# A hybrid attention decoder on one core: the sum of the first squares, a pair of key copies and two remainders put elsewhere in their engines' programs

## The chip, the cores and the metric

The kernel runs on one core of one Trainium2 chip. The metric is the device time of one execution in microseconds, the median of three runs. Engines are named as in the profile: PE is TensorE, DVE is VectorE, ACT is ScalarE, POOL is GpSimd and SP is SyncE.

## What is computed

x is 1 x 1024 x 1024 in float32. Two layers, each of a mixer and a gated feed-forward part, then a last norm:

```
for layer in range(2):
    hn = rms_norm(h, norm_mix_g[layer])
    h = h + hybrid_mixer(hn, ...)      # hn @ w_in, 2 units of dilated attention, 4 of differential, 2 of short convolution, @ w_out
    hn = rms_norm(h, norm_ffn_g[layer])
    g, u = split(hn @ w_up)            # 2816 columns each
    h = h + (silu(causal_dwconv(g)) * u) @ w_down
return rms_norm(h, final_g)
```

Before the mixer's attention, the first quarter of every head's dimensions is turned by angles that come from the positions (sine and cosine tables).

## The kernel before

Features lie on the partitions, the 1024 tokens along the rows. Every float32 operand of a large product is split in two: a head (rounded, `_hi`) and a rest (what is left, `_lo`), and each product is three matmuls: head by head, rest by head, head by rest. A weight block has its head made by a rounding on ACT (line 1825) or POOL, and its rest by a subtraction on POOL (line 762, `rest_of_block`; it writes `w_lo`). When a rest is done, POOL raises `block_ready` (line 765), for which PE waits before it uses the block.

Five engines run programs of their own, written out by hand in Python, and meet by semaphores alone. What stands first in an engine's program is issued first: an instruction that waits holds back everything behind it on its engine.

**The start.** ACT rounds the eight tiles of x of the first half of the tokens to `x_hi` and squares them, then does the same for the second half. DVE makes the rests `x_lo` of the first half (`absorb(0, ...)`), then four tiny products for lambda, then the angles (`angles`, 14 small instructions on 128x128, lines 2580 to 2605), then the rests of the second half (`absorb(1, ...)`), and then `partial(0, 0, 1)`: seven additions (line 2082) that sum the squares of the first half into one tile. PE (`start_normed`, line 1278) sums that tile over the partitions (line 1229), after which DVE takes the roots (`roots(0)`), PE spreads them (line 1275) and ACT keeps them. `partial(0, 1, 1)` and `roots(1)` do the same for the second half. The first projections are under way meanwhile; POOL splits each weight tile (`split`, lines 727 and 729) once PE has freed the place.

**The first unit of attention.** ACT, in the first step of unit 0: it keeps the turned probabilities (line 1693), v, the exponentials of step 1, then copies the second half of q (`keep_q`, lines 1732 and 1733) and of k (`cross_k`, lines 1737 and 1738) to where the score products read them, then the second turned group, and last the head's output (`keep_head`, line 1753).

**The feed-forward part.** The 22 hidden tiles are taken as 11 pairs; products are done in Strassen's manner, with seven instead of eight block products. For each of the first ten pairs of a layer the down projection has four mixed operands, T1 to T4, which POOL forms (line 833, `form`) and ACT rounds (line 1870); POOL then makes their rests (line 837, `rest_formed`). T2 is kept with its sign turned, for which ACT overwrites it after T4 is formed from it (`negate_t2`, line 1876, which raises `t2_negated`). In the program of POOL, for an even tile, these stand in this order:

```
                        form_t2_t3(layer, pair)
                        later_weights(1)
                        form_t4(layer, pair)
                        rest_t3(layer, pair)
                        rest_t2(layer, pair)
                        later_weights(1)
```

Then come `rest_t4` and four more weight blocks. `rest_t3` waits for T3's rounding, `rest_t2` for `t2_negated`. On PE, `part_b` (line 1146) takes the blocks S2, A12, S3, S4, A22 in turn, with four rows of three matmuls each (lines 1126 to 1128); ahead of S2 it waits for the block and for `t_rested` to have counted T1's, T2's and T3's rests together, ahead of A12 for that block:

```
                pe.wait_ge(block_ready, s2 + 1)
                pe.wait_ge(t_rested, 4 * done + 3)
```

DVE, in the same stretch, has two taps of the convolution (line 2491, three operands in SBUF) and the additions to h (line 1989, one operand in PSUM).

Of the kernel before, what the change touches and what calls it, by code (L numbers as in the profile page):

```python
# [18 lines left out]
KT = D_MODEL // P  # L19
# [248 lines left out]
def build(nc, x_t, positions, stream, vectors, first_g, rope, identity, causal, dilation, out_t):  # L268
# [9 lines left out]
    with ctx:  # L278
# [431 lines left out]
        def _(pool):  # L710
# [150 lines left out]
            def form_t4(layer, pair):  # L861
                pool.wait_ge(t_formed, 4 * (layer * (PAIRS - 1) + pair) + 3)
                form("T4", mixed_raw["T2"], k_next[:, 0:HALF])

            def rest_t3(layer, pair):
                pool.wait_ge(t_rounded, 4 * (layer * (PAIRS - 1) + pair) + 3)
                rest_formed("T3")

            def rest_t2(layer, pair):
                pool.wait_ge(t2_negated, layer * (PAIRS - 1) + pair + 1)  # L870
                rest_formed("T2")
# [56 lines left out]
            for layer in range(DEPTH):  # L928
                for n in range(len(PROJECTIONS) + 1):
                    split()  # L930
                    if n == 1:
                        zeros(layer)
                    for name, j in jobs_of_step(n - 3):
                        sum_part(layer, name, j)

                pool.wait_ge(tables_saved, 32)
                pool.wait_ge(next_ready, 2 * (layer + 1) * ATTENDING)
                split_mix(layer, SPLIT_BY_POOL[0])
                pool.wait_ge(half_done, layer * LAYER_HALVES + PROJECTED)
                for m in SPLIT_BY_POOL[1:]:  # L940
                    split_mix(layer, m)
                pool.wait_ge(prob_ready, plain_steps(layer, FINAL, 2))
                for _ in range(len(OUT_TILES) - 3):
                    split()
                sum_ffn(layer)
                split()
                for what, n in feed_forward():
                    pair = (n - 1) // 2
                    if what == "down":
                        later_weights(4)  # L950
                    elif what == "part_a":
                        if n == 0:
                            form_t1(layer, 0)
                            later_weights(1)
                            rest_t1(layer, 0)
                            later_weights(1)
                        else:
                            later_weights(2)
                    elif what == "part_b":
                        rest_t4(layer, n)  # L960
                        later_weights(4)
                    elif n == 0:

                        first_weights(layer)
                    elif n > 1 and n % 2 == 0:
                        later_weights(PRODUCTS - 1)
                        form_t2_t3(layer, pair)
                        later_weights(1)
                        form_t4(layer, pair)
                        rest_t3(layer, pair)  # L970
                        rest_t2(layer, pair)
                        later_weights(1)
                    elif n > 1:
                        later_weights(PRODUCTS - 1)
                        if n < F_TILES - 1:
                            form_t1(layer, (n - 1) // 2)
                        later_weights(1)
                        if n < F_TILES - 1:
                            rest_t1(layer, (n - 1) // 2)
# [575 lines left out]
        def _(act):  # L1555
# [147 lines left out]
            def keep_mix(layer, u):  # L1703
                act.wait_ge(heads_turned, seen(heads_turned))
                by = 1.0 if u < A_UNITS else gain_of(layer, V_SUBLN_SCALED, 0)
                if u >= PENULTIMATE:
                    for t in range(2):
                        act.activation(x_hi[:, u, halves_of_t[t]], bank(IDLE[t]), ACT.Copy, scale=by)\
                           .then_inc(final_hi if u == FINAL else penultimate_hi, 1)
                else:  # L1710
                    if layer:
                        act.wait_ge(h_saved[u], 16 * layer)
                    for t in range(2):
                        act.activation(h[:, u, halves_of_t[t]], bank(IDLE[t]), ACT.Copy, scale=by)\
                           .then_inc(mix_kept, 1)
# [19 lines left out]
            def cross_k(attended, part=slice(0, SEQ)):  # L1735
                act.wait_ge(next_ready, 2 * attended + 2)
                act.activation(k_twice[high, 0, part], k_next[low, part], ACT.Copy).then_inc(hi_kept, 1)
                act.activation(k_twice[low, 1, part], k_next[high, part], ACT.Copy).then_inc(hi_kept, 1)
# [8 lines left out]
            def keep_head(g, i, u):  # L1747
                heads, dilated = heads_of(u), u < A_UNITS
                act.wait_ge(head_done, g + 1)
                act.wait_ge(share_ready, g + 1)  # L1750
                if dilated:
                    for j in range(2):
                        act.activation(heads[:, i, HEAD_DIM * j:HEAD_DIM * (j + 1)],
                                       ps[:, HEAD, HEAD_DIM * j:HEAD_DIM * (j + 1)], ACT.Copy,
                                       scale=share[:, g % 2, j:j + 1]).then_inc(head_out, 1)
                else:
                    act.activation(heads[:, i, :], ps[:, HEAD, 0:P], ACT.Copy, scale=share[:, g % 2, 0:1])\
                       .then_inc(head_out, 1)
                    act.activation(ps[:, HEAD, P:2 * P], ps[:, HEAD, 0:P], ACT.Square,
                                   scale=share[:, g % 2, 0:1], accum_out=head_sums[:, u // FINAL, i:i + 1]).then_inc(head_out, 1)  # L1760
# [14 lines left out]
            def attention(layer):  # L1775
                attended = layer * ATTENDING
                if layer:
                    load_table(ACT.Exp)
                keep_first(layer)
                exps(step_of(layer, 0, 0), 0)  # L1780
                for u in range(ATTENDING):
                    dilated = u < A_UNITS
                    for i in range(QB):
                        g, many = step_of(layer, u, i), len(groups(i, dilated))
                        keep_turned(g, i, dilated, 0)
                        if i == 0:
                            keep_v()
                        if i < QB - 1:
                            exps(g + 1, i + 1)
                        if u == 0 and i == 0:  # L1790
                            keep_q(attended, halves_of_t[1])
                            cross_k(attended, halves_of_t[1])
                        if u < FINAL and i == QB - 2:
                            keep_q(attended + u + 1)
                        if u < FINAL and i == QB - 1:
                            cross_k(attended + u + 1)
                        if u and i == turning_step(u):
                            keep_mix(layer, u - 1)
                        if u == FINAL and i == 0:
                            split_second_channel(layer)  # L1800
                            scale_heads(layer)
                        for n in range(1, many):
                            keep_turned(g, i, dilated, n)
                            if u < FINAL and i == QB - 1 and n == max(1, many - 2):
                                exps(g + 1, 0)
                        keep_head(g, i, u)
                keep_mix(layer, FINAL)

            def conv_center(out, tap):
# [150 lines left out]
        def _(dve):  # L1960
# [16 lines left out]
            def absorb(t, order, g_of):  # L1977
                for m in order:
                    dve.wait_ge(x_hi_ready, seen(x_hi_ready))
                    dve.scalar_tensor_tensor(x_lo[:, m, halves_of_t[t]], h[:, m, halves_of_t[t]], g_of(m),  # L1980
                                             x_hi[:, m, halves_of_t[t]].bitcast(f32),
                                             ALU.mult, ALU.subtract).then_inc(x_lo_ready, 1)
# [653 lines left out]
            for layer in range(DEPTH):  # L2636
                for n in range(2):
# [2 lines left out]
                                      vec[:, layer, c + 1:c + 2], ALU.mult).then_inc(dve_seq, 1)  # L2640
                    dve.wait_ge(dve_seq, seen(dve_seq))
            dve.sem_inc(lam_ready, 1)
            angles()
            absorb(1, range(KT), g_of)
            dve.wait_ge(eye_in, 16)
            partial(0, 0, 1)
            roots(0)
            partial(0, 1, 1)
            dve.wait_ge(rstd_ready, seen(rstd_ready))
# [99 lines left out]
```

## Time and profile before

| what | us |
|---|---|
| median of 3 runs (2380.68 to 2384.05) | 2381.22 |
| the profiled execution's own time | 2382.89 |
| its span | 2381.1 |
| PE busy with matmuls | 2338.4 |
| DVE busy | 1633.0 |
| POOL busy | 1291.0 |
| ACT busy | 990.3 |

The profiled execution is one run, 1.67 us above the median. Its span lies 1.8 us below its own time; that remainder is outside the program's instructions. Busy times of engines overlap. Start times are counted from the start of the span, and "idle before" is the time the engine stood still ahead of an instruction, with what released it behind an arrow.

### The profile page before, as it was taken

How to read it: one execution, taken by the hardware profiler on the slowest of the kernel's cores; microseconds unless marked ns; L12 is line 12 of the kernel's file. 1: busy time of each engine (PE TensorE's matmuls, PEld its weight loads, DVE VectorE, ACT ScalarE, POOL GpSimd, SP SyncE). 2: the span in 40 equal slices, each digit the busy share in tenths (PEclk: the TensorE clock that was granted, in tenths of full speed). 3: DMA queues.
4: the chain of work that ended last, by engine and by line, in shares of the span. 5: the costliest groups of instructions: out<-in, count | busy, mean ns of one | idle time of the engine just before them, and what ended most of it. 6: DMA issues, size and time to landing. Idle time of an engine off the chain costs nothing.

```text
span 2381.1 us, 32322 instructions
## 1 busy us (share of the span) xinstructions
PE 2338.4 (98%) x11340; PEld 1952.4 (82%) x11340; DVE 1633.0 (69%) x2648; ACT 990.3 (42%) x1906; POOL 1291.0 (54%) x893
## 2 busy tenths in 40 slices
PE   7999999999999999999999999999999999999998
PEld 6888888877788888888878888888777888888886
DVE  8744677738767777667795457785496677777775
ACT  4344444525434344344524344444254333433343
POOL 3222323448776667777542223242687777677764
PEclk9999999999999999999999999999999999999999
DMA  8957796421333333333399659852223333333332
GB/s 280 246 140 174 187 223 136 118 62 41 101 95 101 96 96 98 97 94 98 131 282 219 168 145 223 191 105 83 62 67 93 98 96 99 99 94 101 99 100 77
DMA packets 162768, 304.47 MB, mean 128 GB/s; under 512 B 11440, under 2 KB 31024, under 8 KB 162608
## 3 DMA queue, kind: packets, MB, share of 16 engines
q1 hardware_dynamic: 129408, 238.20, 32.3%
q0 software_dynamic: 31616, 62.92, 14.7%
q8 instruction: 92, 1.51, 0.3%
q10 hardware_dynamic: 1584, 1.28, 0.2%
q14 instruction: 68, 0.56, 0.1%
HBM read 292.66 MB, written 135.27 MB: 180 GB/s over the span
## 4 chain that ended last, share of the span: by engine, by line
PE 84%; DVE 8%; POOL 4%; issue 2%; ACT 1%; DMA 1%; DVEq 0%; SPq 0%; POOLq 0%; ACTq 0%
PE ps L1048 11%; PE ps L1049 11%; PE ps L1050 11%; PE ps L1019 7%; PE ps L1021 7%; PE ps L1020 7%; PE ps L1126 5%; PE ps L1128 5%; PE ps L1127 5%; PE ps L1367 5%; PE ps L1354 3%; PE ps L1341 2%; PE ps L1342 2%; POOL w_lo L762 1%; DVE q_next L2082 1%
## 5 line engine op out<-in xcount | busy, mean ns | idle before, releaser
L762 POOL TENSOR_TENSOR w_lo<-more_stage,w_hi 128x512 fp32r<-128x512 f32 x304 | 431.8, 1420 | 193.8 <-ACT w_hi L1825 178.4
L727 POOL CAST w_hi<-stage 128x1024 fp32r<-128x1024 f32 x68 | 71.0, 1044 | 650.1 <-PE ps L1021 575.5
L1019 PE MATMUL ps<-x_hi,w_hi 128*128 128x512 f32 x928 | 373.0, 402 | 2.1 <-POOLq L732 1.0
L1021 PE MATMUL ps<-x_hi,w_lo 128*128 128x512 f32 x928 | 362.9, 391 | 0.0
L1020 PE MATMUL ps<-x_lo,w_hi 128*128 128x512 f32 x928 | 361.6, 390 | 0.0
L1825 ACT ACTIVATE w_hi<-more_stage 128x512 fp32r<-128x512 f32 x294 | 181.8, 626 | 290.2 <-PE ps L1050 205.7
L1989 DVE TENSOR_TENSOR h<-ps,h 128x512 f32<-128x512 f32 x400 | 254.1, 683 | 39.7 <-PE ps L1128 30.1
L1048 PE MATMUL ps<-T_hi,w_hi 128*128 128x512 f32 x688 | 267.9, 389 | 1.5 <-DVE q_next L2457 1.5
L1050 PE MATMUL ps<-T_hi,w_lo 128*128 128x512 f32 x688 | 267.7, 389 | 0.0
L1049 PE MATMUL ps<-T_lo,w_hi 128*128 128x512 f32 x688 | 267.7, 389 | 0.0
L762 POOL TENSOR_TENSOR w_lo<-stage,w_hi 128x512 fp32r<-128x512 f32 x146 | 197.7, 1354 | 128.8 <-ACT w_hi L1825 121.5
L1048 PE MATMUL ps<-B_hi,w_hi 128*128 128x512 f32 x552 | 216.3, 392 | 0.0
L1049 PE MATMUL ps<-B_lo,w_hi 128*128 128x512 f32 x552 | 214.8, 389 | 0.0
L1050 PE MATMUL ps<-B_hi,w_lo 128*128 128x512 f32 x552 | 214.8, 389 | 0.0
L1019 PEld LDWEIGHTS ps<-x_hi,w_hi 128*128 128x128 f32 x928 | 174.5, 188 | 38.8 <-issue 4.4
L1021 PEld LDWEIGHTS ps<-x_hi,w_lo 128*128 128x128 f32 x928 | 174.2, 188 | 38.1
L1020 PEld LDWEIGHTS ps<-x_lo,w_hi 128*128 128x128 f32 x928 | 174.7, 188 | 34.6 <-issue 1.2
L1126 PE MATMUL ps<-mix,w_hi 128*128 128x512 f32 x480 | 187.2, 390 | 3.1 <-POOLq L765 3.1
L1693 ACT ACTIVATE padded<-ps 128x512 f32<-128x512 f32 (+2 forms) x192 | 94.4, 492 | 229.9 <-PE ps L1354 229.8
L1127 PE MATMUL ps<-mix,w_hi 128*128 128x512 f32 x480 | 186.8, 389 | 0.0
L1128 PE MATMUL ps<-mix,w_lo 128*128 128x512 f32 x480 | 186.8, 389 | 0.0
L729 POOL TENSOR_TENSOR w_lo<-stage,w_hi 128x1024 fp32r<-128x1024 f32 x68 | 170.1, 2501 | 5.5
(281 smaller groups left out, 4950.5 us busy)
## 6 DMA issues: line engine op xcount, KB each, us to landing
summed<-stream SPq DMA_DIRECT2D x40, 1024.0 KB, 9.3
more_stage<-stream SPq DMA_DIRECT2D x128, 256.0 KB, 2.7
stage<-stream SPq DMA_DIRECT2D x52, 512.0 KB, 3.9
more_stage<-summed SPq DMA_DIRECT2D x100, 256.0 KB, 2.6
summed_downs<-stream SPq DMA_DIRECT2D x16, 1280.0 KB, 10.6
summed<-stream POOLq DMA_DIRECT2D x20, 1024.0 KB, 15.1
summed<-summed POOLq DMA_DIRECT2D x20, 1024.0 KB, 13.2
more_stage<-summed_downs SPq DMA_DIRECT2D x60, 256.0 KB, 2.6
```

The lines of the kernel that those rows point to most:

```text
L762: pool.tensor_tensor(block_of(w_lo, n), raw, block_of(w_hi, n).bitcast(f32), ALU.subtract)\
L1019: pe.matmul(out, w_hi[:, s, w], hi, start=start, stop=False)
L1020: pe.matmul(out, w_hi[:, s, w], lo, start=False, stop=False)
L1021: return pe.matmul(out, w_lo[:, s, w], hi, start=False, stop=stop)
L1048: pe.matmul(out, block_of(w_hi, n)[:, columns], hi, start=start, stop=False)
L1049: pe.matmul(out, block_of(w_hi, n)[:, columns], lo, start=False, stop=False)
L1050: return pe.matmul(out, block_of(w_lo, n)[:, columns], hi, start=False, stop=stop)
L1126: pe.matmul(bank(b), block_of(w_hi, n)[:, columns], hi, start=start, stop=False, skip_group_check=True)
L1127: pe.matmul(bank(b), block_of(w_hi, n)[:, columns], lo, start=False, stop=False, skip_group_check=True)
L1128: pe.matmul(bank(b), block_of(w_lo, n)[:, columns], hi, start=False, stop=True, skip_group_check=True)\
L1825: act.activation(block_of(w_hi, at), raw_block(layer, n), ACT.Copy).then_inc(block_hi, 1)
L1989: dve.tensor_tensor(row, bank(b), row, ALU.add).then_inc(add_done, 1)
```

## The change

Three edits, each a move within one engine's program; nothing is added or taken away.

- POOL, in each of the 20 pairs with mixed operands: T2's rest now stands ahead of T3's.
- ACT, in the first step of unit 0 of each layer: the copies of k's second half now stand behind the first head's output instead of right behind q's.
- DVE, at the start: the seven additions of the first half's squares now stand ahead of the second half's rests, and the angles behind those.

```diff
@@ -967,8 +967,8 @@
                         form_t2_t3(layer, pair)
                         later_weights(1)
                         form_t4(layer, pair)
+                        rest_t2(layer, pair)
                         rest_t3(layer, pair)
-                        rest_t2(layer, pair)
                         later_weights(1)
@@ -1789,7 +1789,6 @@
                         if u == 0 and i == 0:
                             keep_q(attended, halves_of_t[1])
-                            cross_k(attended, halves_of_t[1])
@@ -1804,6 +1803,8 @@
                         keep_head(g, i, u)
+                        if u == 0 and i == 0:
+                            cross_k(attended, halves_of_t[1])
                 keep_mix(layer, FINAL)
@@ -2640,10 +2641,10 @@
             dve.sem_inc(lam_ready, 1)
+            partial(0, 0, 1)
+            absorb(1, range(KT), g_of)
             angles()
-            absorb(1, range(KT), g_of)
             dve.wait_ge(eye_in, 16)
-            partial(0, 0, 1)
             roots(0)
```

POOL in a pair of the feed-forward part, before, from the forming of T2 and T3 (line 833) on; `mix` and `mix_raw` hold T2 and T3, `t_raw` T4:

```order
L833 TENSOR_TENSOR mix_raw<-k_next,mix_raw 128x512 [waits pool_seq,t_rested,value_ready]
L833 TENSOR_TENSOR mix_raw<-k_next,mix_raw 128x512 [waits b12_kept]
L762 TENSOR_TENSOR w_lo<-stage,w_hi 128x512 [waits block_hi]
L833 TENSOR_TENSOR t_raw<-mix_raw,k_next 128x512 [waits pool_seq,t_formed]
L837 TENSOR_TENSOR mix<-mix_raw,mix 128x512 [waits t_rounded]
L837 TENSOR_TENSOR mix<-mix_raw,mix 128x512 [waits t2_negated]
```

And the same place with the change:

```order
L833 TENSOR_TENSOR t_raw<-mix_raw,k_next 128x512 [waits pool_seq,t_formed]
L837 TENSOR_TENSOR mix<-mix_raw,mix 128x512 [waits t2_negated]
L837 TENSOR_TENSOR mix<-mix_raw,mix 128x512 [waits t_rounded]
L762 TENSOR_TENSOR w_lo<-more_stage,w_hi 128x512 [waits block_hi]
L837 TENSOR_TENSOR t_lo<-t_raw,t_hi 128x512 [waits pool_seq,t_rounded]
L762 TENSOR_TENSOR w_lo<-stage,w_hi 128x512 [waits block_hi]
```

The instruction that waits for `t2_negated` now stands first, and the one that waits for T3's rounding behind it; the block rests (S2's, T4's rest, A12's) follow as before.

DVE at the start with the change, from the products for lambda on (line numbers are one higher than before; `heads` holds the angles):

```order
L2640 TENSOR_TENSOR heads<-vec 128x1 [waits dve_seq] x3
L2083 TENSOR_TENSOR q_next<-k_next,q_next 128x512 [waits dve_seq,squares_ready0]
L2083 TENSOR_TENSOR q_next<-v_next,q_next 128x512 [waits squares_ready0,dve_seq]
L2083 TENSOR_TENSOR q_next<-v_cur,q_next 128x512 [waits squares_ready0,dve_seq]
L2083 TENSOR_TENSOR q_next<-padded,q_next 128x512 [waits squares_ready0,dve_seq]
L2083 TENSOR_TENSOR q_next<-prob,q_next 128x512 [waits squares_ready0,dve_seq] x3
L1981 SCALAR_TENSOR_TENSOR x_lo<-h,gain,x_hi 128x512 [waits x_hi_ready] x8
L2583 CAST heads<-heads 128x128 [waits pos_in]
```

Before, the angles (the cast and the 13 behind it) stood first, then the eight rests, then the seven additions, with the roots behind them; the roots now follow the angles.

## Rows read from the trace of the kernel before

**Rows 1.** The page, its first part: busy time, share of the span, instructions of each engine.
```profile
PE 2338.4 (98%) x11340; PEld 1952.4 (82%) x11340; DVE 1633.0 (69%) x2648; ACT 990.3 (42%) x1906; POOL 1291.0 (54%) x893
```

**Rows 2.** Waits of PE, whole span: total us, times, longest.
```profile
PE ps L1126 <- POOLq L765: 3.1, 4, 1.2
```

**Rows 3.** PE, groups of instructions, 640 to 1180 us: busy, mean ns, idle before.
```profile
L1126 PE MATMUL ps<-mix,w_hi 128*128 128x512 f32 x216 | 84.0, 389 | 0.0
```

**Rows 4.** POOL, timeline around the third pair of layer 0: start, us, instruction, idle before.
```profile
705.02 1.30 POOL L762 TENSOR_TENSOR w_lo<-more_stage,w_hi 128x512 fp32r<-128x512 f32 x1 [1.33 <-ACT w_hi L1825]
...
722.89 3.52 POOL L833 TENSOR_TENSOR mix_raw<-k_next,mix_raw 128x512 f32<-128x512 f32 x2 [0.24 <-POOL w_lo L762]
...
729.08 2.56 POOL L837 TENSOR_TENSOR mix<-mix_raw,mix 128x512 fp32r<-128x512 f32 x2
731.60 1.30 POOL L762 TENSOR_TENSOR w_lo<-more_stage,w_hi 128x512 fp32r<-128x512 f32 x1
733.08 1.29 POOL L837 TENSOR_TENSOR t_lo<-t_raw,t_hi 128x512 fp32r<-128x512 f32 x1 [0.18 <-POOL w_lo L762]
734.32 1.29 POOL L762 TENSOR_TENSOR w_lo<-stage,w_hi 128x512 fp32r<-128x512 f32 x1
735.79 2.06 POOL L762 TENSOR_TENSOR w_lo<-stage,w_hi 128x512 fp32r<-128x512 f32 x1 [0.18 <-POOL w_lo L762]
```

**Rows 5.** ACT, timeline of the same stretch.
```profile
704.31 0.63 ACT L1825 ACTIVATE w_hi<-more_stage 128x512 fp32r<-128x512 f32 x1 [2.09 <-PE ps L1050]
...
729.16 0.63 ACT L1876 ACTIVATE mix_raw<-mix_raw 128x512 f32<-128x512 f32 x1 [1.57 <-POOL t_raw L833]
```

**Rows 6.** PE, timeline: the first rows of S2 and of A12, same pair.
```profile
733.97 0.39 PE L1126 MATMUL ps<-mix,w_hi 128*128 128x512 f32 x1
...
736.69 0.39 PE L1126 MATMUL ps<-mix,w_hi 128*128 128x512 f32 x1
```

**Rows 7.** DVE, timeline of the same pair.
```profile
723.54 1.72 DVE L2042 TENSOR_TENSOR mix<-k_next,mix 128x1024 fp32r<-128x1024 f32 x1
...
734.85 1.85 DVE L2491 SCALAR_TENSOR_TENSOR k_next<-padded,vec,k_next 128x1024 f32<-128x1024 f32 x1
```

**Rows 8.** Line 833 on POOL, all pairs: duration ns least/median/most.
```profile
L833 POOL TENSOR_TENSOR mix_raw<-k_next,mix_raw x40: 1287/1783/2316, 608.7 to 2293.8; 128x512 f32<-128x512 f32 x40
```

**Rows 9.** POOL, DVE and PE, timelines of the first pair of layer 0.
```profile
617.43 1.29 POOL L762 TENSOR_TENSOR w_lo<-more_stage,w_hi 128x512 fp32r<-128x512 f32 x1
...
618.37 1.43 DVE L2491 SCALAR_TENSOR_TENSOR k_next<-padded,vec,k_next 128x1024 f32<-128x1024 f32 x1
...
618.82 0.50 PE L1126 MATMUL ps<-mix,w_hi 128*128 128x512 f32 x1 [1.17 <-POOLq L765]
...
622.30 0.50 PE L1126 MATMUL ps<-mix,w_hi 128*128 128x512 f32 x1 [0.43 <-POOLq L765]
```

**Rows 10.** DVE, timeline of the start.
```profile
17.36 0.23 DVE L2582 CAST heads<-heads 128x128 f32<-128x128 int32 x1
...
21.27 5.39 DVE L1980 SCALAR_TENSOR_TENSOR x_lo<-h,gain,x_hi 128x512 fp32r<-128x512 f32 x8 [0.16 <-DVE heads L2603]
...
29.46 2.76 DVE L2082 TENSOR_TENSOR q_next<-padded,q_next 128x512 f32<-128x512 f32 x1
...
45.01 2.15 DVE L2082 TENSOR_TENSOR q_next<-prob,q_next 128x512 f32<-128x512 f32 x3
```

**Rows 11.** POOL and PE, timelines of the start.
```profile
28.96 2.70 POOL L729 TENSOR_TENSOR w_lo<-stage,w_hi 128x1024 fp32r<-128x1024 f32 x1
...
34.45 1.87 PE L1229 MATMUL ps<-ones,q_next 128*128 128x1 f32 x8 [3.46 <-DVE q_next L2082]
```

**Rows 12.** Busy by stretch: us, PE, PEld, DVE, ACT, POOL, PEclk, DMA share, GB/s.
```profile
34.40:38.00 3.60, 3.54 (x12) 3.20 (x13) 1.36 (x10) 0.00 (x0) 0.00 (x0) 0.50 1.03 380
```

**Rows 13.** PE, timeline of step 1 of unit 0, layer 0.
```profile
78.44 0.43 PE L1367 MATMUL ps<-v_cur,padded 128*128 128x64 f32 x2 [1.68 <-ACT padded L1693]
...
79.29 0.47 PE L1019 MATMUL ps<-x_hi,w_hi 128*128 128x512 f32 x1 [0.19 <-DVE q_next L1966]
```

## The prediction

> **What bounds the kernel now.** I read the page first, then PE's waits, then the timelines of the three places that the change touches. PE is busy for 98% of the span [rows 1], so whatever makes PE stand still is added to the time, and only an idle stretch of PE can be won. Of PE's waits two matter here: 3.46 us at the start for the squares that DVE sums [rows 11], and, in the list by releaser, 3.1 us for weight blocks from POOL, in four places [rows 2]. Those four are two each in the first pair of either layer [rows 9]. In the other pairs PE waits for nobody: the groups of 640 to 1180 us show no idle time ahead of the down rows [rows 3]. The question for POOL's edit is thus how much room the other 18 pairs have.
>
> **POOL: T2's rest ahead of T3's, 20 times.** PE asks for three rests by one count, so T2's rest being early wins nothing: both must be done. What changes is a wait. Before, POOL went from forming T4 (ends about 729.1) straight to T3's rest, and the two rests took 729.08 to 731.64 [rows 4]. ACT turned T2's sign from 729.16 to 729.79 [rows 5], under cover of T3's rest. Now POOL stands at T2's rest until that is done. A POOL instruction that waits for ACT starts 0.08 after ACT's end (704.94 to 705.02, [rows 4, 5]), so the rests start at 729.87 instead of 729.08: 0.79 late, with nothing to hide it on POOL. Queued behind are S2's block rest, T4's rest, A12's and S3's block rests [rows 4].
> - S2: its rest would end at 731.60 + 1.30 + 0.79 = 733.69. PE starts 0.10 after such an end (618.72 to 618.82, [rows 9]), so at 733.79; it came at 733.97 [rows 6]. Covered, by 0.18.
> - T4's rest moves to 733.87 to 735.16.
> - DVE's tap is issued at 734.85 [rows 7], by PE's progress and so as before. Today it falls into A12's block rest, is held until that ends at 735.61 and itself ends at 736.70, 1.09 later. Held behind it, S3's block rest ends at 737.85, 1.15 after the tap [rows 4]. PE has room there.
> - Now the tap falls into T4's rest instead, ahead of A12's. It gets its turn at 735.16 and ends at 736.25; A12's block rest, issued back to back, waits for it and ends at 737.40. PE can start A12 at 737.50 and needs it at 736.69 [rows 6]: a new wait of 0.81.
>
> That DVE goes in between two back-to-back POOL instructions is the step that decides. It is read from forming T2 and T3: together 3.52 instead of twice 1.29 [rows 4], with DVE's 723.54 instruction ending at 725.26, 1.08 after T2's [rows 7]. It is no single case: the median of 40 such POOL instructions is 1783 ns [rows 8], between a short first one and a long second one, in all 18 of the later pairs.
>
> The Trainium skill ("SBUF — State Buffer", section "SBUF: two separate sides") says of the port pair which DVE and GpSimd share that whoever starts first has it for the whole instruction, and speaks of deep queues that the hardware does not drain. Read strictly, POOL's next instruction, already queued, might go first; the sum of this part would then be 1.6 us, not 16.2. The rows above speak for the turn passing to DVE, and I go by them.
>
> So 18 later pairs x 0.81 = 14.6 us. In the first pairs the same shift meets no room: S2's rest now ends at 619.51, and the tap of 618.37 is held until then instead of 618.72 [rows 9], so T4's rest and A12's block rest also come 0.79 late. PE's start of A12 moves from 622.30 to 623.09, its earlier wait for S2 growing by the same 0.79 and not adding to it. Twice 0.8 is 1.6 us. Sum: **+16.2 us**. Bounds: 0 if A12 still comes in time everywhere, and 20 x 1.09 = 21.8 if the whole tap fell on PE.
>
> **DVE: the first squares' sum moved ahead.** Today PE stands 3.46 us for it [rows 11]. Now DVE adds from about 17.4: seven additions at 0.72 ([rows 10]: three in 2.15) end at 22.4. Eight rests at 0.67 [rows 10] end at 27.8, against 26.66 today; PE needs them and comes 1.2 us later, then does 3.6 us of heads and the sums by 32.9 without a wait. POOL's split of the third tile, released by PE, runs 28.7 to 32.9 and holds up DVE: an addition beside it took 2.76 [rows 10, 11]. It now falls on the angles (3.8 us, today 17.36 to 21.11, [rows 10]), which end between 31.6 and 35.5. The roots take 3.1 us, from 33.0 or 35.5. The second sum then meets POOL's next split (35.0 to 39.2) and ends at about 43.8 in both cases, since what is not held in the one is held in the other. Today it ends at 47.16 [rows 10]: 3.3 us won.
>
> Part of that is given back. PE has nothing to do from about 39.3 to 44, which is longer than the 3.46 us after which its granted clock stood at 0.50 [rows 12], 1.2 instead of 2.4 GHz, where sums took 1.87 [rows 11] instead of about 1. A like stretch would now follow the second sum; today's falls where DVE is the slower chain anyway. It takes up to 2.7 us of PE's time, of which PE's chain has about 0.8 to spare before it is the later one. I take 1.3 for it: **-2.0 us**. Bounds: -3.3 (no slow stretch) and +0.5 (the slow stretch hits PE's heads after 27 too, and the second sum comes as late as today). The tables of sine and cosine are issued some 7 us later but still land by 43, 5 us ahead of their use.
>
> **ACT: k's copies behind the first head, twice.** PE's wait of 1.68 us for the turned group [rows 13] goes, since those copies stood ahead of it. But PE's next projection starts at 79.29, when DVE has emptied its bank [rows 13], and DVE waits for none of the moved instructions. PE then waits 2 us for DVE instead. k's copies come 0.7 us later and are asked for two steps on. I take **0**; bounds -1.7 and +0.7 each time.
>
> **Sum:** 16.2 - 2.0 + 0 = +14.2 us. The profiled execution's 2382.89 becomes 2397.1; against the median of 2381.22, which is 1.67 lower, I forecast **2395.4 us**.
>
> **The rivals.**
> - A: POOL keeps its turn. Its next instruction goes ahead of DVE's tap, A12's rest ends at 736.4 and PE finds it ready at 736.69. Then the 18 later pairs cost nothing, and 1.6 - 2.0 = -0.4 leaves 2380.8, not slower. It decides at one point: whether a DVE instruction that waits 0.31 us already gets in. For it: the wait is shorter than the 0.64 in the forming of T2 and T3. Against it: the turn passed each time there. 0.10.
> - B: as forecast, but the start wins nothing, because PE's clock falls in the sparse stretch after 25 or the angles hold up roots and tables. +16.2 to +16.7: 2397.9. 0.15.
> - C: the tap itself comes later than 735.16 in some pairs, or DVE's being done 0.45 earlier is handed on to POOL, so that about half of the waits appear: 8.1 - 2.0 = +6.1, 2387.3. 0.08.
> - D: PE's waits are made good later in the pair, because ACT or DVE is the true limit. Against it, no idle time at all ahead of PE's instructions [rows 3]. Then only the start counts: -2.0 to -3.3, 2378.6. 0.03.
>
> **How the numbers follow.** The forecast has 0.64, B 0.15, C 0.08, A 0.10, D 0.03. The forecast's terms reach from 14.6 + 1.6 - 3.3 = +12.9 to 16.2 + 0.5 = +16.7; widened for PE's wait by 0.15 us a pair (3 us) this is 2391 to 2401. Reaching toward C, I give 2389 to 2400. This measurement can tell about 0.2%, 4.8 us, from no change. Slower by more: forecast, B and most of C, 0.86. Within: A, D and the rest, 0.12. Faster: 0.02.
>
> **What would show it.** PE's waits should name POOL's line 765 ahead of line 1126 some 20 to 24 times, 0.8 us each, at A12; POOL should stand 0.7 us ahead of line 837, released by ACT's line 1876, 20 times; A12's block rest should last over 2 us, and S3's 1.3. At the start PE's wait for the first sum should be gone and that for the second be over 4 us, and the second sum should end near 44. If POOL's A12 rest lasts 1.3 us, the step on the turn is wrong; if PE waits at S2, the room of 0.18 was misread.

## The result, and the profile after

| what | before | after |
|---|---|---|
| median, us (6 runs each, taken together) | 2380.95 (2378.03 to 2384.51) | 2397.32 (2394.93 to 2399.63) |
| the profiled execution's own time, us | 2382.89 | 2398.16 |
| its span, us | 2381.1 | 2396.4 |

The changed kernel is slower: the ratio is 1.0063, with a 95% interval of 1.0053 to 1.0073. That is 15.0 us on 2381.22; the two medians of the table lie 16.4 us apart. Below, a difference from the kernel before is likewise its ratio's share of the median of before, and a difference between two changed kernels is one of medians. The forecast was 2395.4 us with a range of 2389 to 2400 and a chance of 0.86 for slower.

The page of the changed kernel, first part, and below it one line of its list of PE's waits (total us, times, longest). Where line numbers stand behind the change on ACT, they are one higher than before.

```profile
PE 2347.3 (98%) x11340; PEld 1954.3 (82%) x11340; DVE 1645.4 (69%) x2648; ACT 989.9 (41%) x1906; POOL 1305.3 (54%) x893
```

```profile
PE ps L1126 <- POOLq L765: 15.0, 21, 1.9
```

POOL and DVE are busy 14.3 and 12.4 us longer than in [rows 1] with the same number of instructions: they hold each other up for longer. PE's wait for weight blocks was 3.1 us in four places [rows 2], and is now 15.0 in 21. It is there in every pair. Here is PE from 640 to 1180 us, the stretch whose groups had no idle time [rows 3]:

```profile
L1126 PE MATMUL ps<-mix,w_hi 128*128 128x512 f32 x216 | 85.3, 395 | 5.5 <-POOLq L765 5.5
```

POOL's timeline in one pair, the fourth of layer 0; it answers to [rows 4].

```profile
783.16 1.29 POOL L833 TENSOR_TENSOR t_raw<-mix_raw,k_next 128x512 f32<-128x512 f32 x1 [0.18 <-POOL w_lo L762]
785.19 2.56 POOL L837 TENSOR_TENSOR mix<-mix_raw,mix 128x512 fp32r<-128x512 f32 x2 [0.74 <-ACT mix_raw L1877]
787.71 1.29 POOL L762 TENSOR_TENSOR w_lo<-more_stage,w_hi 128x512 fp32r<-128x512 f32 x1
789.17 1.29 POOL L837 TENSOR_TENSOR t_lo<-t_raw,t_hi 128x512 fp32r<-128x512 f32 x1 [0.18 <-POOL w_lo L762]
790.41 2.27 POOL L762 TENSOR_TENSOR w_lo<-more_stage,w_hi 128x512 fp32r<-128x512 f32 x1
792.86 1.30 POOL L762 TENSOR_TENSOR w_lo<-more_stage,w_hi 128x512 fp32r<-128x512 f32 x1 [0.18 <-POOL w_lo L762]
```

DVE and PE in the same pair, from their timelines; the first answers to [rows 7], the second to [rows 6].

```profile
790.16 1.38 DVE L2492 SCALAR_TENSOR_TENSOR k_next<-padded,vec,k_next 128x1024 f32<-128x1024 f32 x1
```

```profile
789.28 0.39 PE L1126 MATMUL ps<-mix,w_hi 128*128 128x512 f32 x1
...
792.79 0.50 PE L1126 MATMUL ps<-mix,w_hi 128*128 128x512 f32 x1 [0.62 <-POOLq L765]
793.12 0.39 PE L1127 MATMUL ps<-mix,w_hi 128*128 128x512 f32 x1
```

This is how the chain reads. POOL stands 0.74 at T2's rest. T4's rest lies at 789.17 to 790.46. The tap of DVE is issued in it, at 790.16, takes its turn when T4's rest ends and is done at 791.54. A12's block rest, begun on paper at 790.41, takes 2.27 instead of 1.29 us: it was held for DVE. It ends at 792.68 and PE starts A12 at 792.79. S2 came without a wait, and S3's block rest takes 1.30, where before it was the held one with 2.06 [rows 4].

At the start, the rows of DVE (timeline) that answer to [rows 10], and PE's and the busy time by stretch that answer to [rows 11, 12]:

```profile
22.20 5.38 DVE L1981 SCALAR_TENSOR_TENSOR x_lo<-h,gain,x_hi 128x512 fp32r<-128x512 f32 x8
...
28.60 0.94 DVE L2591 TENSOR_SCALAR heads<-heads 128x128 f32<-128x128 f32 x1
29.58 3.16 DVE L2594 SCALAR_TENSOR_TENSOR heads<-heads 128x128 f32<-128x128 f32 x3
...
41.05 2.14 DVE L2083 TENSOR_TENSOR q_next<-prob,q_next 128x512 f32<-128x512 f32 x3
```

```profile
31.72 0.95 PE L1229 MATMUL ps<-ones,q_next 128*128 128x1 f32 x8
...
43.25 1.86 PE L1229 MATMUL ps<-ones,q_next 128*128 128x1 f32 x8 [3.64 <-DVE q_next L2083]
```

```profile
44.00:50.00 6.00, 6.00 (x20) 5.01 (x20) 4.76 (x18) 0.00 (x0) 0.00 (x0) 0.60 1.10 269
```

The first sum costs PE no wait any more. The second ends at 43.19 instead of 47.16, PE has stood 3.64 us for it, and the granted clock over 44 to 50 us is 0.60 in the mean, which means that most of them ran at 1.2 GHz.

To see where the time goes between these places I took a mark that all kernels have, the end of ACT's sign change of T2 in each pair, and subtracted its time before from its time after. The differences were -5.26 us in the first pair of layer 0, -3.67 in the second, +4.01 in the tenth; +4.71, +5.49 and +12.92 in the same pairs of layer 1; the span ends at +15.3. From one pair to the next it grows by 0.96 on average in layer 0 and by 0.93 in layer 1 (single steps of 0.90 to 1.17). So the profiled execution won about 5 us at the start, lost 19.4 in the pairs (1.6 and 0.8 in the two first ones, 18 x 0.94 in the others) and about 1 elsewhere. The 5 us hold for this pair of executions: the section on DVE's edit shows that the profiled execution of the kernel before was the slowest of five up to the first pair.

### The profile page after: what moved, and what is told of

The parts are those of the page before. It is cut to its first block, busy times and chain, and to the rows that moved or that the text cites. A ratio compares the mean times of both kernels' runs of the same rounds, so it can differ in the third digit from the quotient of the medians.

```text
span 2396.4 us, 32322 instructions
## 1 busy us (share of the span) xinstructions
PE 2347.3 (98%) x11340; PEld 1954.3 (82%) x11340; DVE 1645.4 (69%) x2648; ACT 989.9 (41%) x1906; POOL 1305.3 (54%) x893
## 3 DMA queue, kind: packets, MB, share of 16 engines
q0 software_dynamic: 31616, 62.92, 14.6%
## 4 chain that ended last, share of the span: by engine, by line
PE 72%; POOL 15%; DVE 7%; issue 2%; ACT 2%; DMA 1%; POOLq 0%; DVEq 0%; SPq 0%; ACTq 0%
PE ps L1048 8%; PE ps L1050 8%; PE ps L1049 8%; PE ps L1019 7%; PE ps L1021 7%; PE ps L1020 7%; POOL w_lo L762 6%; PE ps L1126 5%; PE ps L1367 5%; PE ps L1127 5%; PE ps L1128 5%; POOL mix_raw L833 3%; PE ps L1354 3%; POOL mix L837 2%; PE ps L1341 2%
## 5 line engine op out<-in xcount | busy, mean ns | idle before, releaser
L762 POOL TENSOR_TENSOR w_lo<-more_stage,w_hi 128x512 fp32r<-128x512 f32 x304 | 446.2, 1468 | 194.7 <-ACT w_hi L1826 181.1
```

What stands on the lines that cost most here:

```text
L762: pool.tensor_tensor(block_of(w_lo, n), raw, block_of(w_hi, n).bitcast(f32), ALU.subtract)\
```

## The experiments

Two theories were to be told apart for POOL's edit: that the turn on what POOL and DVE share passes to DVE between T4's rest and A12's block rest (mine), and that POOL is simply later all the way, in proportion to its wait. For the start it was to be seen how much of the won time is given back. Each kernel below was run 11 times, POOL's edit alone 4 times and the filling of 720 elements 5 times. The kernel before was run 27 times beside each of the two groups: their medians are 2382.20 for the first four kernels below and 2382.23 for the last four.

### POOL's edit alone

```diff
                         form_t4(layer, pair)
+                        rest_t2(layer, pair)
                         rest_t3(layer, pair)
-                        rest_t2(layer, pair)
```

> The kernel before with T2's rest ahead of T3's alone. Theory (the tap takes the turn ahead of A12's block rest): PE waits at A12 in each of the 18 later pairs; the two traces give 0.94 us a pair there (period 57.12 before, 58.05 with the change) and about 2.4 us in the two first pairs, so +19 us over before, more than the whole change cost. Rival (my own sum on record): +16. Rival that the start or ACT's edit carries the loss: 0 to +3.

Measured: 2401.92 us (2399.25 to 2403.11), ratio 1.0082 (1.0068 to 1.0096), which is +19.5 us on 2382.20. PE's waits in its profile:

```profile
PE ps L1126 <- POOLq L765: 14.5, 21, 1.9
```

The mark grows by 0.98 us a pair in layer 0 and by 0.95 in layer 1, much as in the changed kernel. POOL's edit alone makes the loss, and more than the whole change lost.

### DVE's edit alone

```diff
+            partial(0, 0, 1)
+            absorb(1, range(KT), g_of)
             angles()
-            absorb(1, range(KT), g_of)
             dve.wait_ge(eye_in, 16)
-            partial(0, 0, 1)
             roots(0)
```

> The kernel before with DVE's edit at the start alone. The traces of before and of the change put DVE's evacuation in step 1 of unit 0 at 78.45 and 73.53, and the first pair at 615.6 and 610.4: theory -5 us, kept to the end. Rival (my sum on record): -2, because the granted clock falls after PE's longer wait for the second sum. Rival that the won time is lost again before the end: 0.

Measured: 2377.43 us (2376.49 to 2380.34), ratio 0.9981 (0.9973 to 0.9990), -4.5 us (interval -6.4 to -2.4). First the two traces, that of before and this one. Before, PE at the second spreading of the roots and at step 1 of unit 0 (beside [rows 13]):

```profile
53.69 1.02 PE L1275 MATMUL ps<-q_next,ones 128*128 128x512 f32 x2
...
61.73 0.47 PE L1019 MATMUL ps<-x_hi,w_hi 128*128 128x512 f32 x1 [0.17 <-DVE q_next L1966]
65.37 0.30 PE L1341 MATMUL ps<-k_twice,q_split 128*128 128x128 f32 x1 [0.68 <-DVEq L2148]
```

With DVE's edit alone, PE at the same two places:

```profile
52.95 1.02 PE L1275 MATMUL ps<-q_next,ones 128*128 128x512 f32 x2
...
75.01 0.47 PE L1019 MATMUL ps<-x_hi,w_hi 128*128 128x512 f32 x1
```

At the spreading only 0.74 us are left of the 3.91 by which the second sum came earlier (43.30 against 47.21, both in PE's timelines): PE is busy all the while, but from 44 to 50 us at a granted clock of 0.50, so the low clock has taken the rest, and more than the 1.3 of the estimate. But at the projection of step 1 PE is 4.28 us ahead (75.01 against 79.29 [rows 13]). In between PE stood before for 0.17 + 0.68 + 1.68 + 0.19 = 2.72 us, three times for DVE and once for ACT, which itself waited for DVE's turned k. With DVE's edit none of the four waits is there.

It would be wrong to put the gain down to these four waits, since other executions with the old order at the start do not have them either. Here is step 1's projection in the kernel with a filling of 310 elements (further below), which leaves the start as it was (its line 1024 is line 1019 of before):

```profile
78.23 0.47 PE L1024 MATMUL ps<-x_hi,w_hi 128*128 128x512 f32 x1
```

And the busy time by stretch, 33 to 55 us, of the kernel before, of that kernel, and of DVE's edit alone (the seventh figure is the granted clock):

```profile
33.00:55.00 22.00, 18.33 (x72) 14.43 (x73) 18.80 (x45) 0.85 (x2) 7.14 (x4) 0.84 0.68 204
33.00:55.00 22.00, 17.88 (x63) 14.20 (x64) 18.85 (x45) 0.60 (x1) 6.77 (x4) 0.77 0.76 221
33.00:55.00 22.00, 18.35 (x68) 14.11 (x67) 19.69 (x54) 3.67 (x7) 6.33 (x4) 0.84 1.06 278
```

Four profiled executions have the old order at the start besides that of before: POOL's edit alone, ACT's edit alone and the two fillings. In all four the mean granted clock of this stretch is 0.77. The clock falls twice there, for 10.2 us together, where the trace of before has one fall of 6.8 us. PE then stands nowhere between 50 and 90 us, and step 1's projection starts at 77.27 to 78.27. The four executions with the new order (DVE's edit alone, it with ACT's, the changed kernel, and A12's rest put first) each have one fall of 6.8 us, and that projection starts at 74.37 to 75.01. Against the four others the new order is thus 3.1 us ahead there, on average, without any of the 2.72. The low stretch after the longer wait is no new cost against them: they had one about the second sum too, and one more before it. At the mark in the first pair of layer 0 the five old orders stand at 613.26 to 615.63, with before the last of them, and the four new ones at 610.38 to 611.27: 3.6 us between the means. Why the clock falls twice in some executions and once in another of the same order is not shown.

### ACT's edit alone

```diff
                             keep_q(attended, halves_of_t[1])
-                            cross_k(attended, halves_of_t[1])
...
                         keep_head(g, i, u)
+                        if u == 0 and i == 0:
+                            cross_k(attended, halves_of_t[1])
```

> The kernel before with k's copies behind the first head alone. Theory: PE no longer waits 1.7 us for the turned group in step 1 but then waits for DVE's evacuation instead, in both layers: 0 us, within 0.5. Rival: the copies held PE up for good, -1.7 to -3.4 us.

Measured: 2381.98 us (2377.24 to 2384.65), ratio 0.9999 (0.9990 to 1.0007). PE's waits in its profile:

```profile
PE ps L1019 <- DVE q_next L1967: 2.3, 2, 2.1
```

In the kernel before, the waits ahead of line 1367 for ACT were 4.0 us, here they are 0.6; those ahead of line 1019 for this DVE line were 0.8, here 2.3. In layer 1 a wait is renamed, as the sum had it: 1.68 for ACT and 0.20 for DVE became 2.15 for DVE. In layer 0 this trace shows neither wait, and nor do three others that have the old start, so they can't show the renaming there. The time says 0, with an interval of -2.4 to +1.7 us.

### A12's block rest ahead of T4's rest

To the changed kernel; POOL does A12's rest before T4's.

```diff
                     elif what == "part_b":
+                        later_weights(1)
                         rest_t4(layer, n)
-                        later_weights(4)
+                        later_weights(3)
```

> The changed kernel, and A12's block rest ahead of T4's rest on POOL in every part b. POOL is as late as in the changed kernel (0.79 us at T2's rest), but the tap now falls into A12's block rest, which so ends in time. Theory of the turn: PE waits at A12 in no later pair, T4's rest is the one that stands behind the tap, where PE has room: -17 us against the changed kernel, about 2379 to 2381. Rival (POOL's lateness as such is paid, wherever it stands): as the changed kernel, 2396.

Measured: 2380.88 us (2378.66 to 2384.95), ratio 0.9997 (0.9988 to 1.0006). POOL's timeline in the fourth pair, and PE's waits:

```profile
783.99 2.56 POOL L837 TENSOR_TENSOR mix<-mix_raw,mix 128x512 fp32r<-128x512 f32 x2 [0.74 <-ACT mix_raw L1878]
786.51 1.29 POOL L762 TENSOR_TENSOR w_lo<-more_stage,w_hi 128x512 fp32r<-128x512 f32 x1
787.98 1.29 POOL L762 TENSOR_TENSOR w_lo<-more_stage,w_hi 128x512 fp32r<-128x512 f32 x1 [0.18 <-POOL w_lo L762]
789.44 2.06 POOL L837 TENSOR_TENSOR t_lo<-t_raw,t_hi 128x512 fp32r<-128x512 f32 x1 [0.18 <-POOL w_lo L762]
```

```profile
PE ps L1127 <- POOLq L765: 3.7, 2, 1.9
```

POOL is as late as in the changed kernel (0.74), and PE waits in no pair but the first of each layer. Lateness in itself costs nothing in the 18; what costs is that the block PE needs next stands behind DVE's turn. With A12 taken out of that place, T4's rest is the held one (2.06), and PE has room for it. It is 16.4 us faster than the changed kernel (2397.32), which is 18 times the 0.94 that its marks grew by, less 0.5. It is still 2.6 us above the change without POOL's edit (2378.30, below). PE's longer waits for blocks in the first pairs, 3.7 us against 1.7 in all, account for 2.0 of that.

### POOL late by less, and by as much, without the edit

To the kernel before is added a filling of an unused tile (`stand`, a memset of `idle_row`), ahead of T3's rest in every pair, of 310 float32 or of 720 bfloat16 elements on 128 partitions. The order of the rests is the old one.

```diff
                         form_t4(layer, pair)
+                        stand()
                         rest_t3(layer, pair)
                         rest_t2(layer, pair)
```

> The kernel before, order unchanged, with one filling of a spare row of 310 float32 on POOL ahead of T3's rest in each pair (about 0.3 us). Theory of the turn: T4's rest then ends about 0.1 us ahead of the tap's start, the tap still falls into A12's block rest, and PE waits nowhere in the 18 later pairs; only the first pairs pay, 0.3 us each: +0.7 us over before. Rival (every lateness is paid in proportion): 20 x 0.3 x 0.94/0.79, +7 us.

> The same with a filling of 720 bf16 (about 0.65 us if it goes by elements). Theory of the turn: T4's rest now ends after the tap has started to wait, so the tap goes ahead of A12's block rest: about 0.8 us a later pair, +14 us, and +2 in the first pairs: +16 us over before, although the order is that of before. Rival (the swap itself, T2's rest ahead of T3's, matters, not POOL's lateness): 0 to +2 us. If the filling turns out shorter than 0.46 us, both say about +1.

Measured: with 310, 2381.79 us (2379.00 to 2384.54), ratio 0.9997 (0.9988 to 1.0006). With 720, 2396.46 us (2395.36 to 2397.16), ratio 1.0060 (1.0048 to 1.0073), +14.2 us (interval 11.4 to 17.4, against 16 expected). POOL's timelines in the third pair, first with 310, then with 720:

```profile
728.62 0.36 POOL L716 MEMSET idle_row<- 128x310 f32 x1
...
732.92 1.29 POOL L841 TENSOR_TENSOR t_lo<-t_raw,t_hi 128x512 fp32r<-128x512 f32 x1 [0.18 <-POOL w_lo L766]
734.17 1.30 POOL L766 TENSOR_TENSOR w_lo<-stage,w_hi 128x512 fp32r<-128x512 f32 x1
735.65 2.05 POOL L766 TENSOR_TENSOR w_lo<-stage,w_hi 128x512 fp32r<-128x512 f32 x1 [0.18 <-POOL w_lo L766]
```

```profile
728.53 0.70 POOL L716 MEMSET idle_row<- 128x720 bf16 x1
...
733.17 1.29 POOL L841 TENSOR_TENSOR t_lo<-t_raw,t_hi 128x512 fp32r<-128x512 f32 x1 [0.18 <-POOL w_lo L766]
734.43 2.28 POOL L766 TENSOR_TENSOR w_lo<-stage,w_hi 128x512 fp32r<-128x512 f32 x1
736.89 1.30 POOL L766 TENSOR_TENSOR w_lo<-stage,w_hi 128x512 fp32r<-128x512 f32 x1 [0.18 <-POOL w_lo L766]
```

DVE's tap in each, from its timeline, first with 310, then with 720:

```profile
734.41 2.14 DVE L2496 SCALAR_TENSOR_TENSOR k_next<-padded,vec,k_next 128x1024 f32<-128x1024 f32 x1
```

```profile
734.29 1.28 DVE L2496 SCALAR_TENSOR_TENSOR k_next<-padded,vec,k_next 128x1024 f32<-128x1024 f32 x1
```

With 310, T4's rest ends at 734.21, 0.20 ahead of the tap. The tap meets A12's rest, which already runs and keeps its turn, and POOL's shift of 0.30 costs nothing. With 720 the tap is issued 0.17 before T4's rest ends at 734.46, and A12's rest is the one held, 2.28 long. PE's waits with 720:

```profile
PE ps L1131 <- POOLq L769: 13.0, 22, 1.8
```

So 0.34 us more on POOL turn a cost of nothing into 14.2 us. A loss in proportion to POOL's lateness would have shown 0.30 / 0.79 of 19.5, some 7 us, with 310; it is excluded by the interval. So the order of the rests plays no part in it: the step comes without the edit as well.

### The change without POOL's edit

DVE's and ACT's edits as in the changed kernel; the two rests of POOL in their old order.

> The changed kernel without POOL's edit, so the start and ACT's edit together. Theory: the sum of the two alone, -4.5 to -5 us against before: 2376 to 2378, faster than before and than the changed kernel. ACT's edit may show now that DVE comes earlier, at most -1 more.

Measured: 2378.30 us (2376.25 to 2380.29), ratio 0.9985 (0.9976 to 0.9993), -3.6 us. It beats both kernels, as does DVE's edit alone; between those two the runs make no difference (2377.43 and 2378.30, ranges that overlap), as ACT's edit would have it.

### The second half's rests ahead of the first half's sum

```diff
-            partial(0, 0, 1)
             absorb(1, range(KT), g_of)
+            partial(0, 0, 1)
             angles()
```

This is an edit of the kernel of the section above.

> As start_and_act, but at the start DVE makes the second half's rests first, then the first half's squares' sum, then the angles. PE then gets the last rest 1 us earlier and still finds the sum about when it asks. Theory (DVE's own chain is the slower one up to the second sum): the same as start_and_act within 1 us. Rival (PE's 1.2 us for the late rests were on the path): 1 us faster.

Measured: 2386.59 us (2382.42 to 2387.83), ratio 1.0014 (1.0005 to 1.0023): +3.3 us against the kernel before (the medians lie 4.4 apart), and 8.3 above the kernel that it was made from. This expectation was wrong. DVE and then POOL in its timelines:

```profile
18.65 5.39 DVE L1981 SCALAR_TENSOR_TENSOR x_lo<-h,gain,x_hi 128x512 fp32r<-128x512 f32 x8 [1.22 <-ACT x_hi L1564]
...
28.92 1.06 DVE L2583 CAST heads<-heads 128x128 f32<-128x128 int32 x1
30.01 2.44 DVE L2585 TENSOR_SCALAR heads<-heads 128x128 f32<-128x128 f32 x1
...
35.10 1.00 DVE L2602 TENSOR_SCALAR heads<-heads 128x128 f32<-128x128 f32 x1
36.13 2.44 DVE L2604 TENSOR_SCALAR heads<-heads 128x128 f32<-128x128 f32 x1
```

```profile
34.98 1.04 POOL L727 CAST w_hi<-stage 128x1024 fp32r<-128x1024 f32 x1 [2.62 <-PE ps L1303]
36.10 2.40 POOL L729 TENSOR_TENSOR w_lo<-stage,w_hi 128x1024 fp32r<-128x1024 f32 x1
```

Three things add up. The rests have to wait 1.22 us for ACT's heads of the second half, a gap that the additions filled in the other order. And because the angles begin 1.26 us later (28.92 against 27.66), their last two instructions are caught by POOL's next split and take 3.44 instead of 0.51 us. The roots begin at 38.79 against 34.55, 4.24 later. In the better order that split falls on the roots, which read and write PSUM and are not held at all (0.16 each throughout), and on one addition (1.47 instead of 0.69).

The third adds most: the tables of sine and cosine are not there when DVE needs them. DVE again, at the first turning:

```profile
50.32 0.69 DVE L2104 TENSOR_TENSOR q_next<-eye,ps 128x512 f32<-128x512 f32 x1
55.33 0.01 DVE L2111 LOAD_MASK_SELECT h<-q_next  x1 [4.33 <-DMA cos_t<-heads]
```

The later angles put off the issue of the tables to between 39.36 and 41.46, and the last landed at 55.30. In the better order they were issued from 35.11 to 37.52, the last landed at 43.56, and DVE did not wait. So 4 us of delay at the issue became 12 at the landing. POOL issues two transfers of its own, here at 39.27 and 40.17, about when the tables are issued, and in the better order at 39.23 and 40.12, behind all of them; whether that is why they land so late is not shown.

PE pays for it three times: it waits 3.7 us for the spreading, 1.7 for the second sum and, behind DVE's wait for the tables, 2.3 for a bank of step 0 at 65.13, in all 4.1 more than the 3.6 of the better order, and after the last of them its clock falls once more. This is the busy time by stretch of the kernel with the rests first, 66 to 72 us:

```profile
66.00:72.00 6.00, 6.00 (x23) 4.88 (x22) 5.72 (x14) 0.88 (x4) 0.00 (x0) 0.72 1.09 247
```

There the better order has a granted clock of 1.00. At the mark in the first pair of layer 0 the two profiled executions are 6.94 us apart (617.33 and 610.39).

## Why the prediction was right, and where two terms were off

- **The step that decides, right.** The tap takes its turn at the end of T4's rest and A12's block rest waits for it (2.27 us). A12 starts 7.67 us after the end of the sign change, against 736.69 - 729.79 = 6.90 before [rows 5, 6]: a wait of some 0.8, forecast 0.81. The recorded wait is 0.62, since the matmul before it is shown to last 0.16 longer than the spacing of the matmuls. The two fillings and A12's rest put first confirm it from both sides.
- **Rival A (POOL keeps its turn) and the strict reading of the rule, wrong here.** The Trainium skill ("SBUF — State Buffer", section "SBUF: two separate sides") has the starter keep the pair for the whole instruction. The rows agree: the tap of 734.41 is held by A12's rest, which began at 734.17. But the section does not say who goes next, and in the 18 pairs no queued instruction of POOL's went ahead of DVE's waiting one; the 1.6 us that the strict reading gave stand against 19.5 measured.
- **The price of a pair, too small.** "18 later pairs x 0.81 = 14.6" measured 18 x 0.94 = 16.9. The wait was sized rightly, but the first matmul after it takes 0.50 instead of 0.39 and the next starts 0.33 after it instead of 0.23; of the remaining 0.13 a pair this restart is 0.10. It could be read before, in the 0.50 of [rows 9].
- **The first pairs.** Forecast 0.8 each; 0.8 in layer 1, but 1.6 in layer 0. There PE's longer wait at S2 (1.85 us) was followed by matmuls spaced 0.43 instead of 0.23 us, at the low clock, from about 615.4 to 618.7. In POOL's edit alone it is the other way round, 0.8 in layer 0 and 1.6 in layer 1, and there the clock fell in the first pair of layer 1. So POOL's term was 16.2 in the forecast and 19.4 in the marks; POOL's edit alone gave 19.5.
- **The start, too small as well.** "3.3 won, 1.3 given back: -2.0" measured -4.5 alone (interval -6.4 to -2.4) and -3.6 with ACT's edit (-5.7 to -1.7). The second sum came 3.97 earlier in the changed kernel, not 3.3. The term that failed is the 1.3 given back. The low stretch came as forecast, but it had to be set against what the old order loses by low clock, and that was read from one trace: 6.8 us of low clock there, 10.2 in four other executions of the same order. Against those nothing is given back; the new order has one low stretch fewer. Against the one trace the 3.2 us that the clock took up to the spreading came back, since the waits that PE had there, 2.72 us, were gone. How far each of the two cases makes the medians is open. The bound of -3.3 lies inside both intervals.
- **ACT, right in what it costs.** The time is unchanged (ratio 0.9999). That the wait for the turned group turns into a wait for DVE is shown in layer 1 alone.
- **The tables.** "Still land by 43, 5 us ahead of their use" was right (42.46 in the changed kernel), but the kernel with the rests first shows how near the edge is: issued 4 us later still, they landed 12 us later and DVE waited 4.33.
- **The sum.** +14.2 was forecast and +15.3 came in the profiled executions. Two errors of about 3 us each (POOL 3.3 too small, the start 2.5 too small a gain), of opposite sign, nearly cancelled; that the total came so close is luck, not precision.
- **The rival C** (half of the waits) did not happen: PE's 21 waits for weight blocks are the 18 pairs, two at S2 in the first pairs, and one at A12 of one of them. POOL stood 14.9 us in 20 places ahead of T2's rest, 0.74 each, as said.

## What to carry to other kernels

Before you move an instruction that waits on an in-order engine, ask what the cover ahead of it was and list everything behind it with the time at which each is needed; here a wait of 0.74 us with nothing of use to anyone in return cost 19.5. Where two engines take turns, as POOL and DVE do here, a delay can cost by steps: look which instruction of the other engine is issued within a few tenths of a microsecond of the boundary, since that decides which of yours is held, and keep the one that is needed next out of that place. Before you build a sum on the waits of one trace, look at a second execution with the same code at that place: here four of five had none of the waits, and lost their time to a low clock instead. And when you move work that ends in a transfer, find the use of that transfer and how long it takes to land among the others.

## What the runs showed of the hardware that was not expected

- POOL's lateness costs by a step: 0.30 us cost nothing (ratio 0.9997), 0.63 us 14.2.
- The tables took 2.7 to 6.0 us each from issue to landing in nine executions and 8.5 to 13.8 in the one where they were issued from 39.36 us on.
- With the same code up to that point, the granted clock fell once at the start in one execution (6.8 us) and twice in four others (10.2 us).
- After a wait of PE the first matmul costs some 0.1 us more than the wait itself (0.50 long, next start after 0.33 instead of 0.23), at the full granted clock.
- Small instructions of DVE with everything in SBUF (a 128x128 cast, free 0.22; a 128x128 operation with a scalar, free 0.29) are held until POOL's instruction ends, to 1.06 and 2.44 us, while those with PSUM among their operands run through the same stretch unchanged at 0.16.
- POOL's filling of a tile took 0.36 us for 310 float32 elements a partition and 0.70 for 720 bfloat16 ones: 1.9 times the time for 2.3 times the elements and 1.2 times the bytes, so nearer to the number of elements.
